# Attention score products of two key groups put in turns, with the query heads held in eight slots 0 1 4 5 2 3 6 7

## The reference, cut to what matters

```python
qb = q.reshape(B, nb, ATT_BLOCK, ATT_KV_HEADS, ATT_GROUP, ATT_HEAD_DIM)
kk = jnp.concatenate([jnp.pad(kb, pad)[:, :-1], kb], axis=2)
s = jnp.einsum('bnqkgd,bnskd->bnkgqs', qb, kk).astype(jnp.float32) * ATT_SCALE
...
p = sink_softmax(s, mask[None, :, None, None], sinks)
o = jnp.einsum('bnkgqs,bnskd->bnqkgd', p.astype(vv.dtype), vv)
...
x = x + jnp.concatenate([o_att, o_ml], axis=-1) @ w_out
```

## Time and profile before

| | |
|---|---|
| median of three runs | 2479.28 us (2477.75 to 2483.95) |
| profiled execution, span | 2481.4 us (its time on the device is not listed apart from the span) |
| attention turns | about 43 to 339 us |
| passage to the mLSTM | about 339 to 397 us |
| mLSTM turns | about 397 to 782 us |
| output projection, feed-forward | the rest |
| TensorE busy | 2396.6 us, 97% of the span |
| VectorE, ScalarE, GpSimd busy | 1628.5, 908.9, 917.9 us |
| mean granted TensorE clock | 0.983 |

### The profile page before, as it was taken

One profiled execution on the slowest core, in us unless ns is written; L12 is line 12 of the kernel. 1 busy time (PEld: TensorE's weight loads), 2 busy tenths in 40 slices (PEclk: granted clock), 3 DMA queues, 4 the chain that ended last, 5 costly groups with the idle time before them and its releaser, 6 DMA issues.

```text
span 2481.4 us, 36492 instructions
## 1 busy us (share of the span) xinstructions
PE 2396.6 (97%) x13782; PEld 2180.3 (88%) x13782; DVE 1628.5 (66%) x2473; ACT 908.9 (37%) x1556; POOL 917.9 (37%) x724
## 2 busy tenths in 40 slices
PE   6999989999998899999999999999999999999999
PEld 5888878999996788788888889999999899999998
DVE  4666663666667334577877786766766866766665
ACT  3444442333333123434334343333333433333232
POOL 3333211212211032563544545434444434434441
PEclk9999989999998999999999999999999999999999
DMA  7322211111114246622222362222222532222221
GB/s 262 150 89 89 76 60 58 60 63 46 55 43 134 87 158 201 219 86 86 86 85 86 98 236 69 69 70 74 66 79 71 180 133 74 67 77 69 69 68 69
DMA packets 150105, 242.85 MB, mean 98 GB/s; under 512 B 17809, under 2 KB 113773, under 8 KB 147901
## 3 DMA queue, kind: packets, MB, share of 16 engines
q1 hardware_dynamic: 149937, 240.93, 28.7%
q0 software_dynamic: 32, 0.07, 0.0%
HBM read 185.08 MB, written 56.84 MB: 97 GB/s over the span
## 4 chain that ended last, share of the span: by engine, by line
PE 56%; DVE 4%; POOL 3%; DMA 2%; issue 1%; ACT 0%; SPq 0%; POOLq 0%; ACTq 0%; DVEq 0%
PE bank L2541 10%; PE bank L2542 10%; PE bank L2543 10%; PE bank L113 8%; PE bank L115 8%; PE bank L114 8%; DMA late_b_raw<-in_w_ffn_in_dram 1%; DVE late_a_lo L2811 1%; PE bank L2484 1%; DVE late_t_lo L2819 0%; DVE late_acc L2873 0%; DVE late_gp L2847 0%; POOL late_t_raw L3008 0%; DVE late_act_lo L2829 0%; DVE late_t L2859 0%
## 5 line engine op out<-in xcount | busy, mean ns | idle before, releaser
L2847 DVE TENSOR_TENSOR late_gp<-bank,late_gp 128x384 f32<-128x384 f32 (+1 forms) x330 | 172.3, 522 | 324.7 <-PE bank L2543 324.5
L2541 PE MATMUL bank<-late_a_hi,late_b_hi 128*128 128x384 f32 (+1 forms) x1056 | 342.4, 324 | 6.3 <-DVE late_b_lo L2819 4.8
L2542 PE MATMUL bank<-late_a_lo,late_b_hi 128*128 128x384 f32 (+1 forms) x1056 | 341.3, 323 | 0.0
L2543 PE MATMUL bank<-late_a_hi,late_b_lo 128*128 128x384 f32 (+1 forms) x1056 | 340.2, 322 | 0.0
L3022 POOL TENSOR_TENSOR late_t<-late_t,late_gp 128x768 f32<-128x768 f32 (+1 forms) x66 | 132.2, 2021 | 505.1 <-DVE late_gp L2847 505.1
L113 PE MATMUL bank<-late_d_hi,late_act_hi 128*128 128x512 f32 (+1 forms) x724 | 283.7, 392 | 5.4 <-DVE late_acc L2873 3.1
L115 PE MATMUL bank<-late_d_hi,late_act_lo 128*128 128x512 f32 (+1 forms) x724 | 282.7, 390 | 0.0
L114 PE MATMUL bank<-late_d_lo,late_act_hi 128*128 128x512 f32 (+1 forms) x724 | 282.5, 390 | 0.0
L2541 PE MATMUL bank<-late_a_hi,late_t_hi 128*128 128x384 f32 (+1 forms) x792 | 259.9, 328 | 12.4 <-DVE late_gp L2847 10.8
L2873 DVE TENSOR_TENSOR late_acc<-bank,late_acc 128x512 f32<-128x512 f32 (+1 forms) x374 | 243.1, 682 | 34.8 <-PE bank L115 34.1
L2542 PE MATMUL bank<-late_a_lo,late_t_hi 128*128 128x384 f32 (+1 forms) x792 | 256.3, 324 | 0.0
(11 more groups left out here) (334 smaller groups left out, 5461.4 us busy)
## 6 DMA issues: line engine op xcount, KB each, us to landing
late_b_raw<-in_w_ffn_in_dram SPq DMA_DIRECT2D x66, 1024.0 KB, 5.1
late_d_raw<-in_w_down_dram SPq DMA_DIRECT2D x32, 1024.0 KB, 4.9
att_next_hh<-h_parts SPq DMA_DIRECT2D x16, 1024.0 KB, 4.8
late_a_raw<-h_parts SPq DMA_DIRECT2D x14, 768.0 KB, 5.4
att_x<-in_x_prompt_dram SPq DMA_DIRECT2D x16, 512.0 KB, 3.6
h_parts<-att_h_hi SPq DMA_DIRECT2D x16, 512.0 KB, 2.7
h_parts<-att_h_lo SPq DMA_DIRECT2D x16, 512.0 KB, 3.4
late_o<-mixed SPq DMA_DIRECT2D x16, 512.0 KB, 4.5
```

What stands on the lines that cost most here:

```text
L2541: nc.tensor.matmul(out, w_h, hi[:, c, :], start=first, stop=False, skip_group_check=True)
L2542: nc.tensor.matmul(out, w_h, lo[:, c, :], start=False, stop=False, skip_group_check=True)
L2543: ins_ = nc.tensor.matmul(out, w_l, hi[:, c, :], start=False, stop=last, skip_group_check=True)
L2847: nc.vector.tensor_tensor(dst, bk, src, ALU.add).then_inc(c_dve, 1)
```

## The change

Eight slots take the heads in the order 0 1 4 5 2 3 6 7. Banks 4 and 5 now take two heads of each key group, and so do banks 6 and 7, and the products switch between the two groups with every product. What belongs to a slot moves with it: the value head, the sinks (four loads of two columns where there was one load of eight), the rows of `w_out` (the first four chunks are read from other rows) and the sample's output, written by 32 transfers of two heads where 16 transfers of four heads did it. The count that waits compare with goes from 16 transfers to 32.

```diff
+SLOT_HEAD = (0, 1, 4, 5, 2, 3, 6, 7)
...
-                sp.dma_start(o_dram[tok:tok + ST, kv * GQ * HD:(kv + 1) * GQ * HD].rearrange("t (j d) -> j t d", j=GQ),
-                             start.os[b4 * 32:(b4 + 1) * 32, 2 * kv + bq, :]).then_inc(start.os_out, 16)
+                for i in range(2):
+                    at = (2 * i + kv) * 2 * HD
+                    sp.dma_start(o_dram[tok:tok + ST, at:at + 2 * HD].rearrange("t (h d) -> h t d", h=2),
+                                 start.os[b4 * 32 + i * 16:b4 * 32 + (i + 1) * 16, 2 * kv + bq, :]).then_inc(start.os_out, 16)
...
-            sp.dma_start(self.w_raw[:, c, :], ins["w_out"][0][c * P:(c + 1) * P, :]).then_inc(self.w_landed[c // 2], 16)
+            row = SLOT_HEAD[2 * c] * HD if c < QW // P else c * P
+            sp.dma_start(self.w_raw[:, c, :], ins["w_out"][0][row:row + P, :]).then_inc(self.w_landed[c // 2], 16)
...
-            (C["sinks"], ins["sinks"][0:1, :].partition_broadcast(P)),
...
+        for n in range(4):
+            at = SLOT_HEAD[2 * n]
+            sp.dma_start(C["sinks"][:, 2 * n:2 * n + 2], ins["sinks"][0:1, at:at + 2].partition_broadcast(P)).then_inc(landed, 16)
...
-                    kv = h // GQ
+                    kv = SLOT_HEAD[h] // GQ
...
-                for b in range(4):
-
-                    if b < 2:
-                        p_kept_a.wait(pe, t - 1, b)
-                    else:
-                        p_kept_v.wait(pe, t - 1, b - 2)
+                parts = (1,) if first else (0, 1)
+                for i in range(2):
+                    for kv in range(HKV):
+                        (p_kept_a, p_kept_v)[i].wait(pe, t - 1, kv)
                     for hh in range(2):
...
-                    scored.mark(ins_)
+                        for pr in parts:
+                            for kv in range(HKV):
+                                half, j = slice(kv * HD, (kv + 1) * HD), 2 * i + hh
+                                ins_ = nc.tensor.matmul(bank[4 + 2 * i + kv][:, hh * 256 + pr * P:hh * 256 + (pr + 1) * P],
+                                                        qT[half, j * P:(j + 1) * P], kT[half, t.p if pr else 1 - t.p, :],
+                                                        start=True, stop=True)
+                                if hh == 1 and pr == parts[-1]:
+                                    scored.mark(ins_)
...
-            sp.wait_ge(start.os_out, 16 * 16)
+            sp.wait_ge(start.os_out, 16 * 32)
```

More of the change, by code:

```diff
@@ L386, in load @@
             sp.dma_start(C["sink_rows"][0:GQ, :], ins["sinks"][0, :].rearrange("(k j) -> j k", j=GQ)).then_inc(landed, 16)
-        self.loads = 16 * 7
+        self.loads = 16 * 10
     def done(self, ins_):
@@ L705, in scores @@
                 k_kept.wait(pe, t)
-                for b in range(4):
-                    if b < 2:
-                        p_kept_a.wait(pe, t - 1, b)
-                    else:
-                        p_kept_v.wait(pe, t - 1, b - 2)
-                    for hh in range(2):
[L713 to L719, removed]
-                    scored.mark(ins_)
+                parts = (1,) if first else (0, 1)
+                for i in range(2):
+                    for kv in range(HKV):
+                        (p_kept_a, p_kept_v)[i].wait(pe, t - 1, kv)
+                    for hh in range(2):
+                        for pr in parts:
[6 more added lines that the diff above has]
+                                    scored.mark(ins_)
             pe.wait_ge(const.built, const.FIRST)
@@ L1669, in period @@
                     weights(t)
-                    act.wait_ge(start.os_out, 16 * 16)
+                    act.wait_ge(start.os_out, 16 * 32)
                     first.round_w(nc, act, range(2))
```

## The result

| | before | changed |
|---|---|---|
| median of the runs beside each other | 2482.86 us (20 runs, 2477.75 to 2487.5) | 2487.73 us (20 runs, 2480.47 to 2491.49) |
| ratio changed / before | | 1.0017 (95%: 1.0009 to 1.0025) |
| profiled execution: span | 2481.4 us | 2488.0 us |
| profiled execution: its own time on the device | not listed | 2490.01 us |
| granted TensorE clock, mean | 0.983 | 0.982 |

A forecast was written before the change was run, and what follows sets the result against it. VectorE's chain with scores and values was taken to bound the attention turns, TensorE the mLSTM. Terms -4.5 (attention) + 8.8 (stall) + 2.0 (clock) = +6.3 us on 2479.28 gave 2485.6 us, range 2473 to 2492.

The forecast's parts named there:

- What bounds: Attention turns: the loop of scores, VectorE with helpers, and values sets the turn, not the full TensorE.
- The scores: Attention scores: paired products take 2.05 us a turn in place of 3.50, freeing 1.45 us of TensorE.
- The attention term: Attention turns: VectorE's second mask comes 0.30 us earlier in each of 15 turns, -4.5 us.
- The stall: Start of the mLSTM: 16 more stores delay tile 2's load, TensorE idles +8.8 us.
- The clock behind it: mLSTM after the idling: granted clock falls to half for a while, +2.0 us, between 1.6 and 4.5.
- Edits at nothing: Extra sink loads, x tile 1.7 us later, `w_out` rows, wait for 32 stores, mask and value work: no cost.
- The sum: Whole kernel: -4.5 + 8.8 + 2.0 = +6.3 us, giving 2485.6 us.
- The base: Starting time: median of the runs taken as 2479.28 us, 2.1 us below the 2481.4 us profiled span.
- half transfers at half the price: Rival, sample's output stores: half transfers issue in half the time, no stall, 2474.8 us; chance 0.22.
- Freed time counts in full: Rival, attention turns: all TensorE time freed, 22.5 us, reaches the end, 2467.6 us; chance 0.04.
- No pairing: Rival, attention scores: products do not run in pairs, 5.6 us lost instead of 4.5 won, 2495.7 us; chance 0.04.
- The clock falls in the attention turns: Rival, attention turns: longer waits lower TensorE's clock in a third of turns, costing 7 us, 2492.6 us; chance 0.12.

The follow-up runs named there:

- run 2: Kernel before, with only its 16 output stores of four heads split into 32 of two heads: 2493.96 us, ratio 1.0043.
- run 1: Changed kernel, with the 32 output stores issued behind the load of mLSTM tile 2 instead of ahead of it: 2477.88 us, ratio 0.9978.
- run 4: Run 1 with each bank's four score products in a row, so the partition half changes once per bank: 2479.31 us, ratio 0.998.
- run 5: Run 1 with VectorE's sum and variance of the next tile's query norm moved earlier: 2469.67 us, ratio 0.9941.
- run 3: Kernel before, with its 16 output stores issued behind the load of mLSTM tile 2: 2483.76 us, ratio 1.0004.
- run 6: Run 3 with VectorE's sum and variance of the next tile's query norm moved earlier: 2470.41 us, ratio 0.9947.

## Why the prediction was right

The forecast was 2485.6 us, +6.3 on the kernel before, within 0.3% as the likeliest; measured are +4.2 us by the ratio (2.2 to 6.2). The two parts can be held against the runs one by one. The loss, 8.8 + 2.0 = 10.8 us, is what run 2 measures alone: 10.7. The gain, 4.5 us, is what run 1 measures alone: 5.5 (2.7 to 8.4). So the small total is not a lucky sum of two wrong parts. Step by step:

- **What bounds.** TensorE 97% busy, yet not the bound of the turn: right. From tile 1 to tile 15 TensorE's busy time fell by 19.3 us and the stretch by 4.4; runs 4 and 5 show it from both sides.
- **The scores.** 3.50 to 2.05 us by the mLSTM's eight records in 0.71: right, 2.06. The price of a pair could be read from another stage of the same program.
- **The attention term**, 15 turns of 0.30: 14 intervals of 0.31 measured, 4.4 us. First mask at the same place, second 0.6 us behind it: right. The wait at the query transposes, forecast near 1.5, is 1.09 us on TensorE and 20.9 / 14 = 1.49 us on its weight loads.
- **The stall**, 8.8 us: right in kind, mis-sized in the profiled execution, 6.9. The 21.3 us of stores were met (the forecast had 32 x 0.664 = 21.2). The term is extra issue time less slack, 10.6 - 1.9; the slack was 10.6 - 6.9 = 3.7 us there. In the passage to the mLSTM this execution had a granted clock of 0.51 from 389.4 to 392.9, where the one before had 1.00 in the same piece of the program. From the first product behind the pause there to the next transposes TensorE takes 5.85 us (388.10 to 393.95), before 4.34 (396.76 to 401.10): 1.5 us more, and SyncE loses nothing. The stall, too, is counted from the end of the last product, which the next one overlaps by 0.35 us where it need not wait. 1.9 + 1.5 + 0.35 is the 3.7. The 1.5 us are a loss that came earlier, not one that was saved. In run 2 the clock stayed at 1.00 in that piece, and the stall was 8.54 us, 0.3 off the term, the same overlap.
- **The clock behind it**, 2.0 us: 2.3 measured (9.2 less 6.9), 2.5 in run 2 (11.0 less 8.54). The stretch at 0.50 was about 4 us, near the lower of the two bounds, as taken.
- **Edits at nothing**: run 1 holds all of them and lacks none of the gain. One of the sinks' loads took 1.97 us to issue in place of some 0.5, so that the x tile behind them moved by 2.9 us (9.92 to 12.78) and not by 1.7, and it stayed covered.
- **The sum.** -4.4 + 6.9 + 2.3 = +4.8 us from the trace's terms, +4.2 by the runs. The profiled executions lie 6.6 us apart in span. At the scores of mLSTM tile 2 they are 1.9 us apart (455.4, 457.3), at the last scores of the mLSTM 3.5 (781.6, 785.1). In between the changed execution had a low clock for 13.7 us near 734 to 748, the one before for 10.3 in the same place, which is worth 1.7 us; no edit is near it. Behind the last scores come 3.1 us more that no edit explains. Run 3, whose code there is that of the kernel before, moves by 1.5 us against it in the same part. The kernel's own runs reach over 11 us (2480.47 to 2491.49), so I leave those 3.1 us unexplained rather than name a cause.
- **The base.** The prediction took the median to lie 2.1 us below the profiled span. In every execution here that lists both, the time on the device is about 2 us above the span, so the profiled execution took about 2483.4 us (an estimate), near the median of the 20 runs. The forecast is a difference to the median and does not suffer by it.

The rivals: *half transfers at half the price* fell with 617 ns. *Freed time counts in full* fell with the 4.4 us. *No pairing* fell with 2.06 us. *The clock falls in the attention turns* fell too: 1.00 from 60 to 320 us, with a wait of over 1 us in every turn. The prediction's sign for it, a clock under 1.00 before 340 us, did appear, from 334.8 us on, but that is the passage: the last attention scores of the prompt tiles start at 328.4 here, and before the first low clock behind them came at 344.4. The Trainium skill (TensorE: Matmul & The Clock Gate, section HAM oscillation) describes a clock that falls in the waits between a loop's bursts; such short waits amid full work did not bring it here.

## What to carry to other kernels

An engine that is 97% busy need not be the bound: look for a small wait that comes back every turn, and count as gain only what moves the chain that the wait shows (0.31 of 1.44 us here); its freed time can pay later, when that chain is made shorter (4.4 us in all became 6.7). A transfer split in two costs its queue two full issues, so before splitting, look at what is queued behind and when it is wanted, and put the load that is wanted first ahead of stores that are not. Loss and gain of nearly the same size look like "no change"; taking each alone turned +0.17% into -0.22% and +0.43%.

## What was not expected of the hardware

- Issue time does not follow size in these stores: 616 ns for 32 partitions and 617 for 16. The eight-partition stores of the earlier trace rows take 295, but they differ in form as well as in size, and the eight-partition transfers within on-chip memory take 625. What sets the price was not tried.
- Products on different partition halves overlap across a change of bank without strict alternation: 2.82 us for 32 records where the half changes once per bank, 2.06 where it changes every time, 3.50 before.
- All ten traces pass through the same piece of the program at the start of the mLSTM: a pause of TensorE of 2.2 to 2.4 us, then work without a pause. In four of them (changed, runs 1, 4 and 6) the granted clock fell just behind it, in the changed execution to 0.51 from 389.4 to 392.9; in the other six, run 2 among them (1.00 from 393.5 to 397.0), it did not. The score order does not sort them. A comparison of single profiles has to allow for about 1.5 us of it.
